# A layer with 64 routed experts: the smaller experts four at a time, their rows by one-hot products

## What is computed

```python
scores = jax.nn.sigmoid(t @ w_router)                 # t: 264 tokens x 1024
biased = scores + router_bias
# 8 groups of 8 experts; the 4 best groups by the sum of their two best; then the 8 best experts
_, eidx = lax.top_k(jnp.where(emask > 0, biased, -jnp.inf), 8)
w = jnp.take_along_axis(scores, eidx, axis=-1); w = w / w.sum(-1, keepdims=True) * 2.5
comb = jnp.sum(jax.nn.one_hot(eidx, 64) * w[..., None], axis=-2)
h = jax.nn.silu(jnp.einsum('td,edf->tef', t, w_gate)) * jnp.einsum('td,edf->tef', t, w_up)
routed = jnp.einsum('tef,efd->td', h * comb[..., None], w_down)   # 64 experts, f = 256
shared = (jax.nn.silu(t @ ws_gate) * (t @ ws_up)) @ ws_down
y = layer_norm(ALPHA * x + routed + shared)
```

## Time and profile before

| | us |
|---|---|
| median of 3 runs (lowest, highest) | 824.35 (823.87, 825.01) |
| the profiled execution, its own time | 824.56 |
| its span | 822.8 |
| TensorE busy in it | 805.0 |

### The profile page before, as it was taken

How to read it: one execution, slowest core, us unless ns; L and a number is a source line. 1 busy time by engine, 2 the same in 40 slices (tenths; PEclk the granted TensorE clock), 3 DMA queues, 4 the chain that set the end, 5 groups by cost and what they waited for, 6 DMA issues and landing times.

```text
span 822.8 us, 11931 instructions
## 1 busy us (share of the span) xinstructions
PE 805.0 (98%) x4283; PEld 500.9 (61%) x4283; DVE 465.1 (57%) x1178; ACT 166.1 (20%) x275; POOL 93.1 (11%) x105
## 2 busy tenths in 40 slices
PE   9999999999999999999999999999999999999995
PEld 7876788888788888544545445454544445445443
DVE  6989899999741367533434334443444434334356
ACT  2210112111221005321211212121121212112126
POOL 1119700000010002100000000000000000000021
PEclk9999999999999999999999999999999999999998
DMA  9432344445489946699999999999999999999981
GB/s 333 151 128 103 122 139 149 155 154 115 142 321 417 414 182 249 219 397 416 423 423 420 423 425 424 422 427 420 425 425 423 424 426 424 420 424 419 419 351 53
DMA packets 45372, 262.15 MB, mean 319 GB/s; under 512 B 9928, under 2 KB 10696, under 8 KB 26256
## 3 DMA queue, kind: packets, MB, share of 16 engines
q1 hardware_dynamic: 40720, 252.88, 76.6%
q0 software_dynamic: 4608, 8.66, 2.8%
HBM read 267.10 MB, written 2.53 MB: 328 GB/s over the span
## 4 chain that ended last, share of the span: by engine, by line
PE 83%; DMA 9%; SPq 6%; DVE 1%; issue 1%; ACT 1%; ACTq 0%; DVEq 0%
PE banks L1263 35%; PE banks L1474 21%; PE banks L1518 10%; PE banks L1435 6%; DMA high<-w_gu 5%; SPq L464 4%; DMA ring<-w_gu 4%; PE banks L1410 3%; SPq L472 2%; PE banks L1364 1%; PE banks L1278 1%; PE banks L1495 1%; PE banks L1290 1%; PE banks L1440 1%; DMA ring<-w_front 1%
## 5 line engine op out<-in xcount | busy, mean ns | idle before, releaser
L1474 PE MATMUL banks<-high,low 128*64 128x512 f32 x848 | 230.1, 593 | 0.9 <-DMA high<-w_gu 0.9
L1263 PE MATMUL banks<-xT,ring 128*128 128x264 f32 x768 | 176.3, 389 | 0.3 <-DMA ring<-w_front 0.3
L1170 DVE TENSOR_TENSOR cgb<-cgb,banks 128x264 f32<-128x264 f32 x248 | 89.8, 423 | 132.1 <-PE banks L1435 131.9
L1263 PEld LDWEIGHTS banks<-xT,ring 128*128 128x128 f32 x768 | 144.5, 190 | 30.4 <-issue 5.5
L1474 PEld LDWEIGHTS banks<-high,low 128*64 128x64 f32 x848 | 73.6, 137 | 138.6 <-issue 135.1
L1222 DVE SCALAR_TENSOR_TENSOR y_pair<-banks,sml,y_pair 128x1024 fp32r<-128x1024 f32 x31 | 39.8, 1284 | 121.8 <-ACT y_pair L725 121.8
L1474 PE MATMUL banks<-ring,low 128*64 128x512 f32 x176 | 77.6, 593 | 3.0 <-DMA ring<-w_gu 3.0
L562 POOL DMA_INDIRECT low<-x_rows_dram,idx x32 | 31.9, 997 | 423.5 <-DVE idx L1114 403.0
L1435 PEld LDWEIGHTS banks<-sw,y_pair 128*128 128x128 f32 x496 | 63.0, 188 | 24.9 <-issue 23.5
L1518 PE MATMUL banks<-high,mu 128*64 128x512 f32 x336 | 77.0, 599 | 0.7 <-ACT mu L705 0.7
L1435 PE MATMUL banks<-sw,y_pair 128*128 128x264 f32 x496 | 71.1, 293 | 0.0
(11 more groups left out here) (300 smaller groups left out, 859.9 us busy)
## 6 DMA issues: line engine op xcount, KB each, us to landing
high<-w_gu SPq DMA_DIRECT2D x35, 2048.0 KB, 24.0
high<-w_dn SPq DMA_DIRECT2D x40, 1024.0 KB, 21.9
ring<-w_front SPq DMA_DIRECT2D x78, 512.0 KB, 3.2
high<-w_gu SPq DMA_DIRECT2D x34, 1024.0 KB, 11.5
ring<-w_gu SPq DMA_DIRECT2D x7, 2048.0 KB, 28.8
us<-w_dn SPq DMA_DIRECT2D x11, 1024.0 KB, 21.8
ring<-w_gu SPq DMA_DIRECT2D x8, 1024.0 KB, 12.0
bgb<-w_dn SPq DMA_DIRECT2D x6, 1024.0 KB, 21.4
```

The lines of the kernel that those rows point to most:

```text
L1170: dve.tensor_tensor(acc[:, n], acc[:, n], psum[:, bank, 0:T], ALU.add).then_inc(added, 1)
L1263: ins = pe.matmul(psum[:, 6 + n % 2, 0:T], ring[:, n % RING, k], rhs[:, k], start=(k == 0), stop=(k == KC - 1))
L1474: ins = pe.matmul(psum[SL * j:SL * j + SL, GU_BANK, :], xg[:, k, SL * j:SL * j + SL], gu[slots[j]][:, k], start=(k == 0), stop=(k == KC - 1))
```

## The change

**Order.** Places take the part of expert numbers. Experts 0 to 7, whose weights are loaded before the routing is known, keep places 0 to 7. The other 56 are ranked by the number of their rows: the six largest stand at places 8 to 13, the 24 smallest at 14 to 37, the rest at 38 to 63 in rising order. The ranks are made in step 0: the key row is turned into a column, compared, and the ranks become a permutation matrix `places`; the gates and picks are transposed, multiplied by it and counted again. SyncE reads an expert's number from `order` before it loads it.

**Steps.** Steps 0 to 6 take a pair, steps 7 to 12 four experts with 32 places each (output in quarters of the partitions), steps 13 to 25 a pair: 26 in place of 32. Were one of the 24 longer than 32 rows, or another longer than 64, further rounds follow. Ahead of each step of four stand 14 products of the identity with itself whose output nobody reads.

**Rows.** The rows of steps 7 to 16 don't come by an indirect transfer: GpSimd widens `S` to float32 (`S32`), and TensorE multiplies the token rows, which stay in SBUF (`xcb`, where `dn_7` was; the sample tokens' rows in `sample_rows`), by it (`gather_rows`). These products stand in steps 6 to 15, where the turn was.

```diff
-        DOWN_PAIRS = ((4, 5), (0, 1), (2, 3), (7, 5), (0, 1), (2, 3))
+        DOWN_PAIRS = ((4, 5), (0, 1), (2, 3))
+        QUAD_FROM, QUAD_TO = 14, 38
+        IDLE_PRODUCTS = 14
...
-                sp.wait_ge(x1_scaled, KC)
-                sp.dma_start(dn[7], w_dn[6]).then_inc(dn_in[7], 16)
...
+                refill(0, 0, SLOT_PAIRS[0], DOWN_PAIRS[0], [6, 7], halves=True)
+                sp.wait_ge(order_ready, 1)
+                static = PER_TURN + 2 * QUADS + 1
+                for it in range(1, static):
+                    refill(it, step_of(it), SLOT_PAIRS[it % 3], DOWN_PAIRS[it % 3], [2 * it + 6, 2 * it + 7], halves=it < EARLY_HALVES, by_place=True)
...
                 sp.wait_ge(lists_ready, 1)
-                refills = sp.value_load(rounds[0:1, 1:2], min_val=TURNS - 1, max_val=MOST - 1)
...
+                def widen(step, u):
+                    pool.wait_ge(select_ready, step + 1)
+                    pool.wait_ge(turned, step)
+                    pool.sem_inc(rows_moved, 1)
+                    pool.tensor_copy(S32, S[:, u]).then_inc(widened, 1)
...
+                def gather_rows():
+                    def columns(k):
+                        return psum[:, 2 + k // 4, (k % 4) * P:(k % 4) * P + P]
+
+                    for k in range(KC):
+                        for c in range(2):
+                            pe.matmul(columns(k), xrow[c][:, k * P:k * P + P], S32[:, c], start=(k % 4 == 0 and c == 0), stop=False)
+                    for h in range(HC):
+                        for g in range(2):
+                            rows = slice(32 * g, 32 * g + NS)
+                            ins = pe.matmul(columns(HC * g + h), sample_rows[rows, h * P:h * P + P], S32[rows, 2], start=False, stop=(h == HC - 1))
+                    ins.then_inc(turned, 1)
...
+                def sort_gates():
+                    pe.wait_ge(sort_inputs, GATES_COPIED)
+                    pe.wait_ge(sort_inputs, RANKED)
+                    pe.wait_ge(shared_h, FC)
+                    for c in range(TC):
+                        pe.matmul(psum[:, SORT_BANKS[1], c * P:c * P + P], turned_gates[:, c], places, start=True, stop=True)
+                    pe.matmul(psum[0:1, SORT_BANKS[1], TC * P:TC * P + E], tokid[0:E, 0:1], places[0:E, 0:E], start=True, stop=True).then_inc(sort_products, 1)
...
+                    size = 2 * SL // len(slots)
+                    if len(slots) == 4:
+                        keep_warm(IDLE_PRODUCTS, GU_BANK)
                     pe.wait_ge(xg_ready, it + 1)
...
-                            ins = pe.matmul(psum[SL * j:SL * j + SL, GU_BANK, :], xg[:, k, SL * j:SL * j + SL], gu[slots[j]][:, k],
+                            ins = pe.matmul(psum[size * j:size * j + size, GU_BANK, :], xg[:, k, size * j:size * j + size], gu[s][:, k],
                                             start=(k == 0), stop=(k == KC - 1))
...
+                        if before is None and k == 1:
+                            turn_gates()
+                        if before is None and k == 4:
+                            sort_gates()
                     ins.then_inc(gu_done, 1)
+                    if before is None:
+                        count_sorted()
...
-                        turn()
+                        if wide is None:
+                            turn()
+                        else:
+                            gather_rows()
```

More of the change, by code:

```diff
@@ L488, in _, with step_of, expert @@
[L488 to L491, removed]
+                        sp.dma_start(dn[s], w_dn[bass.ds(e, 1)].rearrange("o p f -> (o p) f")).then_inc(dn_in[s], 16)
+                def step_of(pair):
+                    return pair if pair <= PER_TURN else PER_TURN + 1 + (pair - PER_TURN - 1) // 2
+                def expert(place):
+                    return sp.value_load(order[0:1, bass.ds(place, 1)] if not isinstance(place, int) else order[0:1, place:place + 1], min_val=0, max_val=E - 1)
@@ L492, in _ @@
+                with sp.Fori(0, middle) as q:
+                    for i in range(PER_TURN):
+                        later_refill(q, i, refill)
+                for i in range(LATE_HALVES):
+                    later_refill(middle, i, refill, halves=True)
+                later_refill(middle, LATE_HALVES, last_refill)
                 for h in range(KC // 2):
@@ new lines, in count_sorted @@
+                def count_sorted():
+                    pe.wait_ge(sort_inputs, SORTED_PICKS)
+                    for c in range(TC + 1):
+                        for b in range(min(c + 1, TC)):
+                            rows = slice(0, tok[b])
+                            before = (tri_spread[rows] if b == 2 else tri16[:]) if b == c else ones16[rows]
+                            ins = pe.matmul(psum[:, SORT_BANKS[0], c * E:c * E + E], before, pk[rows, b], start=(b == 0), stop=(b == min(c, TC - 1)))
+                    ins.then_inc(sort_products, 1)
@@ L1457, in banks_added, with visit @@
                     pe.wait_ge(added, first + (last + 2))
-                def visit(it, u, slots, downs, loaded, halves, first_down=None, before=None, gathers=None, shared=(), by_halves=True):
+                def visit(it, u, pairs, loaded, halves=None, before=None, ahead=None, gathers=None, wide=None, shared=()):
+                    last = ahead is None
+                    it_sorted = isinstance(it, int) and it == FIXED // 2 - 2
+                    slots = [s for r in pairs for s in SLOT_PAIRS[r % 3]]
+                    downs = [s for r in pairs for s in DOWN_PAIRS[r % 3]]
+                    loads = [n for n in loaded for _ in range(2)]
+                    size = 2 * SL // len(slots)
+                    if len(slots) == 4:
+                        keep_warm(IDLE_PRODUCTS, GU_BANK)
@@ L1477, in visit @@
                             ins.then_inc(gu_mid, 1)
-                            if gathers is None:
+                            if last:
                                 pe.wait_ge(y_split, it)
@@ L1547, in _, with loads_of @@
-                visit(0, 0, SLOT_PAIRS[0], DOWN_PAIRS[0], 16, 1, 16, gathers=16)
-                turn_of_pairs(0)
-                turn_of_pairs(1, shared=True)
-                earlier = pe.value_load(rounds[0:1, 1:2], min_val=TURNS - 1, max_val=MOST - 1)
-                with pe.Fori(2, earlier) as q:
+                def loads_of(pair):
+                    return 16 * (pair // 3 + 1)
+                visit(0, 0, [0], [16], halves=1, ahead=(4, 2), gathers=16)
+                for k in range(1, 1 + PER_TURN):
+                    ahead = (2 * k + 4, 2) if k + 2 <= PER_TURN else (QUAD_FROM + 4 * (k + 1 - PER_TURN), 4)
+                    visit(k, k % 2, [k], [loads_of(k)], halves=1 + k // 3, before=KC * (k - 1), ahead=ahead,
+                          gathers=16 * ((k + 1) // 2 + 1), wide=k + 1 if k == PER_TURN else None)
@@ new lines, in _ @@
+                pe.wait_ge(rows_stored, 16 * (TC + 2))
+                for k in range(1, 1 + QUADS):
+                    pairs = [PER_TURN + 2 * k - 1, PER_TURN + 2 * k]
+                    ahead = (QUAD_FROM + 4 * (k + 1), 4) if k + 2 <= QUADS else (QUAD_TO + 2 * (k + 1 - QUADS), 2)
+                    visit(PER_TURN + k, k % 2, pairs, [loads_of(r) for r in pairs], before=KC * (PER_TURN + k - 1), ahead=ahead, wide=PER_TURN + k + 1, shared=SHARED_AT[k])
+                turns = n_turns(pe)
```

392 lines of the change are left out of this document (275 added, 117 removed).

## The result

| | before | after |
|---|---|---|
| median of 12 runs each, us | 824.22 | 826.45 |
| lowest, highest | 823.62, 825.01 | 824.18, 827.99 |
| the profiled execution, its own time (span) | 824.56 (822.8) | 824.87 (823.1) |

The ratio is 1.0026, with a 95% interval of 1.0018 to 1.0034. The changed kernel is a quarter of a per cent slower: 2.2 us, 1.45 above the forecast of 825.0 and 0.45 above the band of 822.7 to 826.0 that the prediction called no change. Its runs spread over 3.8 us, those of before over 1.4.

The account below looks back on a forecast made before the run. Transfers were taken to bound the kernel until the sixth step of four (590.0), TensorE after: 590.0 + 20.0 + 55.5 + 126 plus 2 for the clock put the last pair at 793.5, giving 825.0 us; range 819.5 to 832.

Parts of the forecast that it names:

- four abreast: Gate-up and down in a step of four: four experts cost what two did, gate-up 6.87 us, down 3.58.
- The row products: One-hot products replacing the turn in steps 6 to 15: 5.53 us against 1.06, 4.47 more per step.
- The sort: Ranking the experts within step 0's gate-up: adds 1.1 us to TensorE.
- Step 2, the hole: First step of four ends at 469.3; only then is pair 10's down transfer issued, leaving transfers idle 0.8 us.
- Step 1: Transfers ahead of the steps of four: pair 9's down weights land at 460.6, pair 10's gate and up end at 470.5.
- c = 2: Slow-clock cost in the sixth step of four's gate-up: 2 us taken, bounds 0 and 6.87.
- the waits swallow that: Third to fifth steps of four: a gate-up started at the low clock costs nothing, as TensorE waits for weights.
- transfers last: Rival: transfers, not TensorE, still set the end of the routed stage; 819.9 us, or 821 to 822; chance 0.22.
- two abreast: Rival: steps of four run their products only two at a time, 10.4 us more a step; 859 us; chance 0.03.
- the extra round: Rival: one of the 24 experts exceeds 32 rows, adding a round of 547 us; 1372 us; chance 0.01.
- all of the bytes: Rival: no hole in the transfers, TensorE never last, the byte saving shows in full; 817 us; chance 0.03.
- The clock and dearer row products: Rival: slow clock costs 5 us at the sixth step of four, row products 5.4 more a step; 831.7 us; chance 0.19.

Follow-up runs that it names:

- the two profiles: The changed kernel's first profiled execution, 824.87 us, and the same kernel run once more with no edit for a second profile, 826.93 us.

## Why the prediction was nearly right

Point by point, against its numbered sum, for the profiled run:

- *What it rests on* held: four abreast; waits for weights from the third to the sixth step of four, though shorter than the 7 us of the forecast (6.0 ahead of the third, 3.5 to 3.9 ahead of the others, where the slow gate-up before took part of it); TensorE last behind the sixth, with nothing to spare where it was tried (6.42 of 6.45).
- *The row products* were dearer in the forecast than on the chip: 3.80 + 1.09 = 4.89, not 5.53; the term of 4.47 is 3.8 by these records, 4.0 by the length of a step. Three pairs with them took 666.63 - 612.46 = 54.2, not 55.5.
- *The sort* was too cheap: step 1 starts 2.2 later than before, not 1.1. With 1.1 us more in steps 1 to 5 together and 4.0 for the row products, step 6 ends at 447.58 instead of 445.7, and the first step of four at 470.72 instead of 469.3.
- *Step 2, the hole,* is what failed: 0.8 us in the sum, 4.2 on the chip. The sum counted the hole at pair 10's down matrices alone. It took pair 10's gate and up weights to follow pair 9's down matrices without a gap. Step 1 had the last of these in at 460.6, and it came at 460.8; but with only that matrix left in the queue the rate was already 217 GB/s. For the slots of pair 10 come free only when the first step of four has done its gate-up, which is late by the sort, by the row products of step 6 and by 3.32 of idle products: they were issued at 458.12. Take out the idle products, and this hole is gone (451 GB/s); take out the row products, and it is gone as well (430). The later end of that step (470.72 for 469.3) then widened the second hole. On TensorE itself these idle products cost nothing, since the third step waits for its weights in any case; on the transfers, with the row products in place, they cost 3.3 us. So the sixth step starts at 592.78, not 590.0.
- *The clock.* c = 2 was taken; it is 1.7 or 0, by the run. The prediction's "the waits swallow that" for the third to fifth steps held.
- The sum came out at 793.5 for the last pair's start, the two profiles at 793.19 and 795.25. That the first is so near is luck: the sixth step starts 2.8 late, and the missing c of 2 and the cheaper row products (1.3 in the three pairs) make up for it. In the second, near the median, c is there, and that is about the 1.45 us by which the forecast was low.

Of the rivals, transfers last, two abreast, the extra round and all of the bytes did not come. The clock and dearer row products is half there: the clock is, at a third of its price, the row products are cheaper than forecast. The Trainium skill, "TensorE: Matmul & The Clock Gate", HAM oscillation, which stood behind it, has a burst that waited for its weights start slow, every time. The traces agree for the gate-up of every third, fourth and fifth step of four of these two profiles and of one of the two sixth ones, seven of eight, though in three of the seven the clock fell only 0.2 to 1.3 us after the burst had begun. The same page of the Trainium skill, Measured speedup vs the span model, has 3.07 times for four row tiles and 2.38 for three column tiles. The traces don't agree for four column tiles: 64 records in 7.00 us beside 32 in 6.87 are twice the rate of two abreast.

## What to carry to other kernels

Work that keeps an engine busy on purpose belongs only where that engine would wait for data anyway and where a slow start would reach the end; ahead of steps that still have data in store it delays the release of their buffers, and if the queue is nearly drained by then, as it was here with the row products, the transfers pay for it. When two resources are nearly balanced, a saving on one shows only up to the other's slack: with one step of row products less, 3.9 us, the last pair started 2.7 earlier (789.79 to 787.09), 0.8 of the rest being a wait for weights and 0.4 the later end of the sixth gate-up. So price a trade between them (bytes for products) stage by stage: here it was free where TensorE waited for weights anyway, by the argument above, and worth next to nothing in the pairs. A term that hangs on the clock is a spread as well as a mean, so look at more than one profile of a kernel before explaining a microsecond.

## What was not expected of the hardware

The length of TensorE's rest did not decide whether the clock fell. In the first profile after, it did nothing from 588.9 to 592.78 (3.9 us) and the granted clock stayed at 1.00 through the gate-up that followed; in the second it did nothing from 589.6 to 593.11 (3.5 us), and the clock fell to 0.50 when it had already begun again, for about 3 us. So a rest of this length is paid in some runs of the same kernel and not in others. Shorter ones show the same: with 28 idle products ahead of that step the rest was 1.76 us in one kernel and the clock stayed at 1.00 (gate-up 7.05), and 1.99 us in another, where it fell to 0.50 about 1.3 us into the burst (8.75; the run with steps 14 to 16 gathered).
